# A hybrid encoder block on one core: the token sums of the last block made behind the recurrence's projections

## The reference

```
h = rmsnorm(x) * norm1_w;  p = h @ w_in            # 2816 columns in seven parts
A = sliding-window attention with QK-norm, partial rotary, sinks   (8 heads of 64)
B = HGRN2 gated linear recurrence in chunks of 64 tokens           (4 heads of 128)
    state = exp(b_last) * state + (k * exp(b_last - b))^T v        # chunk by chunk
x = x + concat(A, B) @ w_out
h = rmsnorm(x) * norm2_w
x = x + (silu(h @ w_gate) * (h @ w_up)) @ w_down
```

## Time and profile before

| | us |
|---|---|
| median of 3 runs | 2267.28 |
| lowest and highest run | 2266.98 and 2268.28 |
| span of the profiled execution | 2265.8 |
| TensorE busy in it | 2201.5 (97%) |
| VectorE busy | 1259.6 (56%) |
| ScalarE busy | 928.9 (41%) |

### The profile page before, as it was taken

How to read it: one execution, slowest core, us unless ns; L and a number is a source line. 1 busy time by engine, 2 the same in 40 slices (tenths; PEclk the granted TensorE clock), 3 DMA queues, 4 the chain that set the end, 5 groups by cost and what they waited for, 6 DMA issues and landing times.

```text
span 2265.8 us, 31421 instructions
## 1 busy us (share of the span) xinstructions
PE 2201.5 (97%) x12640; PEld 1905.6 (84%) x12640; DVE 1259.6 (56%) x1902; ACT 928.9 (41%) x1674; POOL 132.3 (6%) x138
## 2 busy tenths in 40 slices
PE   7999999999999988999999999999999899999999
PEld 7889988998899878888888888888888788888887
DVE  4675467547644775666666676555555334343433
ACT  4773376347634842433333343333333223223232
POOL 2101201020102001000000000000000000000000
PEclk9999999999999999999999999999999999999999
DMA  3312332232132246433333242222221445454453
GB/s 134 135 72 94 115 129 75 93 127 107 69 131 94 103 159 226 174 116 132 132 132 132 84 154 82 83 82 83 84 84 66 167 147 183 177 188 179 176 191 135
DMA packets 83584, 284.52 MB, mean 126 GB/s; under 512 B 8624, under 2 KB 17072, under 8 KB 68848
## 3 DMA queue, kind: packets, MB, share of 16 engines
q1 hardware_dynamic: 72176, 234.02, 28.9%
q0 software_dynamic: 11264, 48.50, 5.8%
HBM read 227.96 MB, written 54.53 MB: 125 GB/s over the span
## 4 chain that ended last, share of the span: by engine, by line
PE 58%; DMA 1%; DVE 1%; issue 0%; ACT 0%; SPq 0%; DVEq 0%; ACTq 0%; POOLq 0%
PE b_bank_A L248 4%; PE b_bank_A L250 4%; PE b_bank_A L249 4%; PE b_bank_C L248 4%; PE b_bank_C L250 4%; PE b_bank_B L250 4%; PE b_bank_B L248 4%; PE b_bank_B L249 4%; PE b_bank_C L249 4%; PE b_hx_bank L1453 3%; PE b_hx_bank L1454 3%; PE b_hx_bank L1455 3%; PE b_bank_D L248 2%; PE b_bank_D L249 2%; PE b_bank_D L250 2%; PE b_hx_bank L1402 1%
## 5 line engine op out<-in xcount | busy, mean ns | idle before, releaser
L1471 DVE TENSOR_TENSOR b_dn_lo<-b_dn_stage,b_dn_hi 128x1024 fp32r<-128x1024 f32 x88 | 107.8, 1226 | 305.2 <-ACT b_dn_hi L1351 305.1
L248 PE MATMUL a_pj<-a_w_hi,a_hT_hi 128*128 128x256 f32 x896 | 259.0, 289 | 1.7 <-issue 1.7
L249 PE MATMUL a_pj<-a_w_lo,a_hT_hi 128*128 128x256 f32 x896 | 253.4, 283 | 0.0
L250 PE MATMUL a_pj<-a_w_hi,a_hT_lo 128*128 128x256 f32 x896 | 253.3, 283 | 0.0
L1351 ACT ACTIVATE b_dn_hi<-b_dn_stage 128x1024 fp32r<-128x1024 f32 x88 | 93.3, 1060 | 344.7 <-PE b_bank_D L1455 310.2
L924 DVE TENSOR_TENSOR a_w_lo<-a_w_stage,a_w_hi 128x2048 fp32r<-128x2048 f32 (+1 forms) x64 | 137.9, 2155 | 72.9 <-ACT a_w_hi L587 72.9
L248 PEld LDWEIGHTS a_pj<-a_w_hi,a_hT_hi 128*128 128x128 f32 x896 | 171.5, 191 | 6.6 <-issue 4.4
L249 PEld LDWEIGHTS a_pj<-a_w_lo,a_hT_hi 128*128 128x128 f32 x896 | 171.7, 192 | 0.0
L250 PEld LDWEIGHTS a_pj<-a_w_hi,a_hT_lo 128*128 128x128 f32 x896 | 171.5, 191 | 0.0
L1453 PE MATMUL b_hx_bank<-b_dn_hi,b_a_hi 128*128 128x512 f32 x352 | 138.2, 393 | 6.8 <-DVE b_a_lo L1471 6.7
L248 PE MATMUL b_bank_A<-b_h_hi_B,b_w_hi 128*128 128x512 f32 x352 | 137.8, 392 | 0.0
(11 more groups left out here) (272 smaller groups left out, 5548.5 us busy)
## 6 DMA issues: line engine op xcount, KB each, us to landing
a_w_stage<-w_whole SPq DMA_DIRECT2D x56, 1024.0 KB, 4.8
b_gu_stage<-w_gu SPq DMA_DIRECT2D x44, 1024.0 KB, 5.2
b_dn_stage<-w_dn SPq DMA_DIRECT2D x88, 512.0 KB, 3.3
a_mid<-b_a SPq DMA_DIRECT2D x88, 256.0 KB, 4.2
b_a_stage<-a_mid SPq DMA_DIRECT2D x88, 256.0 KB, 3.6
b_hx<-hc POOLq DMA_DIRECT2D x13, 1024.0 KB, 5.1
a_x_res<-x_pad POOLq DMA_DIRECT2D x16, 512.0 KB, 5.3
x_mid<-a_x_res POOLq DMA_DIRECT2D x16, 512.0 KB, 3.4
```

What stands on the lines that cost most here:

```text
L248: pe.matmul(out, stationary[0](k), moving[0](k), start=(k == 0 and not adds), stop=False, skip_group_check=adds)
L249: pe.matmul(out, stationary[0](k), moving[1](k), start=False, stop=False, skip_group_check=adds)
L250: last = pe.matmul(out, stationary[1](k), moving[0](k), start=False, stop=(k == ends), skip_group_check=adds)
L1471: dve.tensor_tensor(out, full, hi.bitcast(F32), ALU.subtract).then_inc(ready, 1)
```

## The change

The mix steps move in the list, and the places of their stores and loads in SyncE's queue move with them. Nothing is added or taken away.

```
--- before
+++ after
@@ block_steps
-    after("Q23", 1, ("mix", 0, 0))
-    after("I23", 1, ("mix", 0, 1))
-    after("I23", 3, ("mix", 1, 0))
-    after("G23", 0, ("mix", 1, 1))
+    after("G23", 3, ("mix", 0, 0), ("mix", 0, 1))
     for n in range(CHUNK_AT["WO0"], NW):
         after(chunk_name(n), 1, ("split_lo", n + 1))
-    after("WO0", 2, ("mix", 2, 0), ("mix", 2, 1))
-    after("WO1", 3, ("mix", 3, 0), ("mix", 3, 1))
+    after("WO0", 2, ("mix", 1, 0), ("mix", 1, 1))
+    after("WO1", 2, ("mix", 2, 0), ("mix", 2, 1))
+    after("WO2", 2, ("mix", 3, 0), ("mix", 3, 1))
@@ SyncE, in the loop over chunks
-                if b == NB - 1 and n in (CHUNK_AT["G23"], CHUNK_AT["WO0"] + 1):
-                    p = 0 if n == CHUNK_AT["G23"] else 1
+                if b == NB - 1 and n in (CHUNK_AT["WO1"], CHUNK_AT["WO2"], CHUNK_AT["WO3"]):
+                    p = n - CHUNK_AT["WO1"]
                     store_mixed(sp, hc, 0, p, mix_x, mix_t, mixed, 3 * p, hc_stored)
                     load_mix(p + 1)
 
-        store_mixed(sp, hc, 0, 2, mix_x, mix_t, mixed, 6, hc_stored)
-        load_mix(3)
         sp.wait_ge(w_lo_ready.sem, w_lo_ready.upto(NB - 1, NW - 2))
```

## The result

The changed kernel takes 2271.31 us (median of 17 runs, 2269.79 to 2274.5), the kernel before 2267.52 us (17 runs, 2265.6 to 2269.93): a ratio of 1.0018, 95% interval 1.0012 to 1.0025. It is slower by 2.7 to 5.7 us; the middle of that, 4.1 us, lies just under the 4.5 us (0.2%) that the prediction took as the least difference to be told. The forecast of the time was 2270.7 us. In block 2, ahead of everything that the edits touch, the traces stand up to 0.8 us apart from that of the kernel before (the split behind `a_w_lo` starts at 561.84 us there, at 561.04 in experiment 9 and 562.54 in experiment 7), so a time that differs by less says nothing by itself.

What follows compares the result with a forecast made beforehand. TensorE, busy 97%, was taken to bound the kernel through its waits. The 8.5 us removed were outweighed by the one-buffer mixing chain and tail, last sum 898.3 against 894.94: 2267.28 + 3.4 = 2270.7 us, range 2267.6 to 2275.5.

Steps and rivals of the forecast that it cites:

- What the change removes, 8.5 us: Block 3, head 2's increments to head 3's outputs: without mixing it takes what block 2's stretch takes, 8.5 us less.
- (1) the stall ahead of yt 3: Mixing 0 on VectorE delays `yt 3`'s low part; TensorE stalls 3.8 us, inside the buffer's chain, not on top.
- (2) the chain: Mixings 0 to 3 share one pair buffer; each waits for store and reload, links of 13.7, 14.5 and 14.5 us.
- the columns' chain: GpSimd's column store and reload behind mixings 2 and 3: forecast in time for the sums, covered by about 1 us.
- (3) who waits: From mixing 1 VectorE's loads set the pace; TensorE stalls 3 to 4 us, then some 3 us at each other mixing.
- the text on the clock: Slow-clock rival's remark: a fall at an earlier stall costs nothing, as the chain has 3 us to spare a chunk.
- (4) the tail: After mixing 3 ends at 889.0: remaining sums take 3.6 + 5.7 us, stage A's last sum at 898.3 against 894.94.
- (5) costed at nothing: WO2/WO3 weights, column store and reload, pair 3's stores, old SyncE steps: all taken as covered, 0 us.
- The slow clock in the tail: Rival: TensorE's 3.1 us idle before mixing 3's end halves its clock, costing 3.4 us more: 2274.1 us, chance 0.26.
- The chain that keeps up: Rival: pair stores and loads are hidden, TensorE keeps all but the 3.8 us stall: -4.7, 2262.6 us, chance 0.04.
- its low bound: Whole kernel, with pair loads of 4.8 us three times: +1.8 us instead of +3.4.

Runs made afterwards that it cites:

- experiment 9: Kernel before the change, mix steps where they stood, with a second pair buffer so that pair 1 is loaded early: 2263.12 us, ratio 0.9980.
- experiment 7: Changed kernel, one pair buffer kept, with own buffers for the residual columns of WO2 and WO3 in the last block: 2270.62 us, ratio 1.0015.
- experiment 1: Changed kernel with mixing 0 moved behind the sums of WO0's groups 0 and 1, instead of ahead of `yt 3`: 2276.44 us, ratio 1.0041.
- experiment 2: Changed kernel with a second buffer for the pairs, pair 1 loaded early, and an own semaphore for `a_mix_t`'s store: 2272.47 us, ratio 1.0021.
- experiment 5: experiment 2 with own, early-loaded buffers for the residual columns of WO2 and WO3 in the last block: 2264.09 us, ratio 0.9984.
- experiment 3: Changed kernel with the edits of experiment 1 and experiment 2 together: 2267.57 us, ratio 1.0002.
- experiment 4: Changed kernel, one pair buffer, the next load waiting only for the stores that read `a_mix_x`, not for `a_mix_t`'s: 2270.66 us, ratio 1.0015.
- experiment 8: experiment 2 with mixing's stores and loads one chunk later in SyncE's queue, WO2's and WO3's weights issued ahead of them: 2268.22 us, ratio 1.0001.
- experiment 6: experiment 5 with mixing 0 moved behind the sums of WO0's groups 0 and 1: 2265.14 us, ratio 0.9985.

## Why the prediction was right

It said 2270.7 us, a last sum at 898.3 and +3.4 us; measured were 2271.31, 898.34 and +3.40 (3.8 by the medians). The mechanism came true, the wait of the one buffer's chain; that the last sum agrees to 0.1 us is in part luck: the chain began 0.3 us earlier than forecast and its three links were 0.3 us longer together (42.96 us for 42.7). By its steps:

- *What the change removes, 8.5 us.* Right: head 3's outputs come 8.7 us earlier, 16.8 us behind head 2's increments (17.1 forecast), and mixing 0 starts at 840.67 for 841.0. Block 2 was a good image of block 3 without mixing. Experiment 9 shows it from the other side: with the pair in place early, the old order too wins 4.8 us by the medians, while 3.09 us of the wait and a clock at half behind it are left.
- *(1) the stall ahead of yt 3.* Right: 3.82 us for 3.8. That it isn't on top of the chain was shown by experiment 1, where its removal made the kernel slower.
- *(2) the chain.* Starts forecast 841.0, 854.7, 869.2, 883.7; measured 840.67, 854.40, 869.26, 883.63. The loads were 4.8, 5.9 and 5.4 us for 4.8, 5.6 and 5.6. Experiments 2, 5 and 7 together show that this chain rules the changed kernel: to cut it alone gives nothing, since the columns' chain lies just under it, to cut the columns' chain alone gives nothing either, and to cut both gives 7.2 us against the changed kernel. By the fit of the Trainium skill ("DMA: Bandwidth & Descriptors", the section on one DMA's anatomy) the loads would be 4.4 us by an estimate and the sum +1.5; the trace is 2 us above it, so the rows were the better source. The section gives that fit for DMAs that GpSimd issues, and these loads stand in SyncE's queue, which the prediction didn't say.
- *(3) who waits.* Right in kind, wrong in size: the stalls were 1.80, 3.10 and 1.11 us for "3 to 4" and "some 3 us at each of the others". The step took TensorE at full clock between them. It was at half behind two of the stalls, so it came later to the bank and stood shorter; the chain's spare time swallowed that, as the text on the clock said it could.
- *(4) the tail.* Right: 898.34 - 889.0 = 9.3 us.
- *(5) costed at nothing.* Right, but thin: WO0's columns were stored and their buffer was loaded again by 866.95 + 6.2 = 873.2, and the sum that needs it stood behind mixing 2's end at 874.6. The next reload took 6.8 us, more than the 6.3 that the step had as the most, and landed by 880.73 + 6.8 = 887.5, ahead of 888.9, as the store before it had been quicker. The prediction had this margin as "about 1 us" and didn't ask what becomes of it if the first chain gets shorter. In experiments 2, 3, 4 and 8 that became the limit.
- *The rivals.* The slow clock in the tail (2274.1 us, 0.26) did not come in the profiled execution: the tail's idle was 1.11 us, since a fall behind the stall at 875.03 had made TensorE late (VectorE waited 4.39 us for a sum at 879.69). That is the case in which the prediction says that the fall costs nothing. In experiment 1 it did come, behind an idle of 2.38 us, and cost 1.5 us: the clock was at half for 3.4 us, not for the 6.9 that the rival carried over from the idle of 7.75 us. So its price of 3.4 us was more than twice the measured one. And the length of the idle does not decide it, as the rival took it to: in experiment 7 TensorE resumed in the tail behind an idle of 2.75 us with the clock full. The single runs of the changed kernel reach to 2274.5. The six longest have a mean clock of 0.993, and of the nine below 2271.5 us three have 0.993 and six 0.994; that fits more time at half in the longer ones, but doesn't show where. The chain that keeps up (2262.6) needed both chains cut: experiment 5 is that kernel, at 2264.09. The range begins at 2267.6, which the prediction calls just below its low bound; that bound, +1.8, is 2269.1.

The first expectations behind the prediction did worse than the prediction itself. For experiments 2 to 4 they took the tail as free once the pairs' chain was shorter, and missed by up to 9 us. What failed was the same step (5), used outside the kernel for which it had been worked out. Experiment 6 missed by 5 us for another reason, the order in VectorE's own queue.

## What to carry to other kernels

A step that is moved takes its loads, its stores and its single buffer along: add up one round of use, store and reload (here 13.7 to 14.9 us) and compare it with the time of the work that it is laid beside (11.4 us), before looking at how busy the engine is. When a wait is cut and nothing is won, look for the next transfer through a reused buffer, and for what its DMA now shares its microsecond with or finds still under way. A stall that stands inside a longer chain can be removed with no gain, or with a loss if the chain starts later for it.

## What the runs showed of the hardware

- A store of 512 KB in GpSimd's DMA queue, issued 1.4 us behind a mixing store of 768 KB that took its usual 3.5 to 3.8 us, landed after 4.0 to 5.4 us where no load was issued within 2 us (5.1 in the changed kernel), 8.6 us with a load of 1024 KB issued in SyncE's queue in the same 0.1 us, and 10.3 to 10.8 us with 2048 KB of loads within 0.5 us. The weights' load in that company took 10.2 to 10.7 us, against 7.5 to 8.1 in the same kernels (experiments 2, 4 and 5) behind a pair's load without the store.
- The pair's load of 1024 KB took 4.8 us where it was issued once the mixing's stores had landed and no column store was under way. Issued 1.5 us behind a mixing store still under way it took 5.4 to 6.1 us without the column store (experiments 2, 4, 5 and 8) and 5.8 to 6.4 us with it.
- The granted clock fell to half behind idles of 3.8 and 3.1 us, for 3.3 and 3.4 us each; around and behind the 7.75 us of the kernel before it was half for 6.9 us, and around the 3.83 us of experiment 5 for 6.8 us. Whether it falls is not told by the length of the idle alone: behind the 1.80 us in the changed kernel it stayed full, while in experiment 7 it was 0.72 in 862 to 868 us, behind an idle of 1.83 us, and full in 890 to 896 us, behind one of 2.75 us.
